# Turning the triangular inverse on VectorE and moving the sixteen spare keys of a query block, in a one-core hybrid attention and RWKV-7 block

## Chip, core and metric

One core of a Trainium2 chip runs the whole block for one batch of 512 tokens. The metric is the time of one execution on the device in microseconds (us), the median of the runs. One more execution was recorded with the hardware profiler; all rows below come from it. PE is TensorE, PEld its weight loads, DVE is VectorE, ACT is ScalarE, POOL is GpSimd, SP issues DMAs.

## What is computed

Sixteen meta tokens are put before 512 tokens of width 1024. After an RMS norm and one input projection, two branches of eight heads of 64 run beside each other and are merged by gates; a second half is a gated feed-forward net.

```python
def sb_block(q_blk, q_pos, k, v):            # stick-breaking attention
    z = einsum('bhqd,bhsd->bhqs', q_blk, k) * HEAD_DIM ** -0.5
    visible = arange(T)[None, :] < q_pos[:, None]
    nl = where(visible, softplus(z), 0.0)
    between = cumsum(nl, reverse=True) - nl
    weights = where(visible, exp(log_sigmoid(z) - between), 0.0)
    return einsum('bhqs,bhsd->bhqd', weights, v)

def step(S, inp):                            # RWKV-7, one token
    sa = einsum('bhvk,bhk->bhv', S, -kk_t)
    S = S * w_t + sa[..., None] * (kk_t * a_t)[:, :, None, :] + v_t[..., None] * k_t[:, :, None, :]
    y = einsum('bhvk,bhk->bhv', S, r_t)

merged = sigmoid(gate_sb) * (o_sb @ w_branch_sb) + sigmoid(gate_rw) * (o_rw @ w_branch_rw)
h = h + rms_norm(merged @ w_out, norm_mix_post)
f = (silu(f @ w_ffn_gate) * (f @ w_ffn_up)) @ w_ffn_down
h = h + rms_norm(f, norm_ffn_post)
```

## The kernel before

The kernel goes through four stretches. Up to about 186 us it norms, transposes and projects (26 weight units of 1024x128, each split into a high and a low part so that three fp32r products stand for one fp32 product) and prepares the operands of both branches. From 186 to 370 us lies the mix stage, which is what the change is about. Then come the late part (`LATE`: gates of the RWKV branch, group norm, remaining gate units, branch projections), the output projection and the feed-forward net.

In the mix stage four kinds of work share the engines. Their steps are written out by hand in four lists, `ORDER_PE`, `ORDER_ACT`, `ORDER_DVE` and `ORDER_POOL`; each engine runs its list in order, and steps wait for each other over the counting semaphores `mix_pe`, `mix_act`, `mix_dve`, `mix_pool`. Names are kind, number, step, as `i2.W3`.

- `i` (inv), batches 0 to 4 of two chunks of 64 tokens (the last has one): the inverse of a unit triangular 64x64 matrix for eight heads, by doubling. `A` and `L` form the matrices. At level j, `W` multiplies the matrix by the current inverse X (tile `xx`), ACT copies the product to SBUF (`w`), `Y` multiplies the transposed X by that, and DVE writes the new blocks into X under a mask (`x`, COPY_PREDICATED). The transposed X comes from `R`: PE multiplies X by an identity into PSUM, and ACT copies that to `xt` (`xt0` to `xt4`). Up to level 4, X is block diagonal in blocks of 32; at level 5 the result itself goes to `xt`, from where `SA` reads it. POOL presets X with the identity (`ident`).
- `s` (seq), nine chunks: the recurrence. `F`, `RB` form products, DVE masks them (`aak`, `ark`, `arb`), `T0` to `T2` transpose on PE, ACT copies `bh` and `kh`, DVE copies `v`, then `Z1`, `Z`, `SA`, `OUT1`, `OUT`, `S` with the copies `z`, `sa`, `out` on ACT and `decay`, `s` on DVE.
- `a` (att), four pairs of heads: scores `Q0` to `Q2`, sigmoids on ACT (`z`, `m`), masks on POOL (`b`, `c`), running products on DVE (`S`), weights on DVE (`w`, and `t` for 16 keys of each query block), transposes `X0` to `X5` with ACT copies, `X6` (four transposes of the 16 keys) with an ACT copy to `wmeta`, and `O`: two matmuls of 512 columns with the 16 keys (`vmeta`), then the 128-key tiles. A query block of 128 sees 16 + 128(i+1) keys, so 16 are left over beside whole tiles of 128; here they are the meta tokens, the last of the reversed row.
- `g` (gate), ten weight units: each is four pieces of 6 matmuls of 512 columns (`G0` to `G3`) into bank `GBANK`; ACT and DVE split the next unit (`hi`, `lo`), DVE copies the sums to `gate_raw` (`raw`), SP writes them to HBM. `u0.U` is one more gate unit of 24 matmuls.

Work of 64x64 tiles goes through `heads`, whose matmuls run on quadrants of PE: for pairs p of 2 and 3 the operand or the result lies in the other half of the partitions, which `rows` decides. That is line 1553 of the profile; 32x32 tiles (level 5) are line 1582. A logical fp32 matmul shows as two MATMUL records.

## Time and profile before

| | |
|---|---|
| median of 3 runs | 865.57 us (863.52 to 865.91) |
| the profiled execution's own time | 865.65 us |
| its span in the profile | 863.7 us |
| busy in the span: PE | 847.9 us, 98% |
| PE weight loads | 706.4 us, 82% |
| DVE | 463.9 us, 54% |
| ACT | 350.8 us, 41% |
| POOL | 104.4 us, 12% |
| PE share of the chain that ended last | 93% |
| granted TensorE clock | full speed in all 40 slices |

The page gives busy time by engine and the chain of work that ended last, followed back from the last instruction. Matmuls are pipelined, so their durations overlap; how long a row of them takes is read from start to start in the timeline. A line of the timeline is start, duration, engine, line of code, operation, tile written and tiles read, shape, count.

### The profile page before, as it was taken

To read this page: it belongs to the slowest core of one execution; us is meant where nothing else is said; L and a number is where in the kernel's file an instruction comes from. 1 tells how busy PE (TensorE), PEld (TensorE's weight loads), DVE (VectorE), ACT (ScalarE), POOL (GpSimd) and SP (SyncE) were. 2 spreads that over 40 slices of the span, in tenths; PEclk is the share of its full clock that TensorE was granted. 3 is DMA by queue.
4 is the path that set the end of the run, shared out by engine and by line. 5 is a ranking of instruction groups with operands and counts; after the bars stand their busy time and mean duration, and the time that the engine had idled before them with its cause. 6 is when DMAs were issued, how large, how long until landed. Compare 5 with 4: busy or idle time off the path is not lost.

```text
span 863.7 us, 18793 instructions
## 1 busy us (share of the span) xinstructions
PE 847.9 (98%) x8125; PEld 706.4 (82%) x8125; DVE 463.9 (54%) x593; ACT 350.8 (41%) x520; POOL 104.4 (12%) x106
## 2 busy tenths in 40 slices
...
DMA packets 109584, 82.61 MB, mean 96 GB/s; under 512 B 3471, under 2 KB 100025, under 8 KB 109258
## 3 DMA queue, kind: packets, MB, share of 16 engines
...
q14 instruction: 13, 0.11, 0.0%
...
## 4 chain that ended last, share of the span: by engine, by line
PE 93%; DVE 4%; ACT 1%; issue 1%; DMA 0%; DVEq 0%; SPq 0%; ACTq 0%
PE psum L583 48%; PE psum L1804 19%; PE psum L1553 8%; PE psum L1609 7%; PE psum L1847 2%; PE psum L1445 2%; PE psum L1727 1%; DVE w_lo L573 1%; PE psum L1744 1%; PE psum L1758 1%; DVE shift_diff L1149 1%; PE psum L1436 1%; DVE k_mod L1190 1%; DVE v_t L1154 1%; PE psum L1520 1%
## 5 line engine op out<-in xcount | busy, mean ns | idle before, releaser
L573 DVE TENSOR_TENSOR w_lo<-w_raw,w_hi 128x1024 fp32r<-128x1024 f32 x69 | 90.3, 1309 | 119.1 <-ACT w_hi L568 114.7
L583 PE MATMUL psum<-f_hi,w_hi 128*128 128x512 f32 x336 | 130.8, 389 | 0.0
L583 PE MATMUL psum<-f_lo,w_hi 128*128 128x512 f32 x336 | 130.7, 389 | 0.0
L583 PE MATMUL psum<-f_hi,w_lo 128*128 128x512 f32 x336 | 130.7, 389 | 0.0
L1391 DVE TENSOR_TENSOR w_lo<-w_raw,w_hi 128x1024 fp32r<-128x1024 f32 x44 | 53.9, 1226 | 125.5 <-ACT w_hi L1061 121.4
L1061 ACT ACTIVATE w_hi<-w_raw 128x1024 fp32r<-128x1024 f32 x44 | 46.7, 1061 | 166.6 <-PE psum L583 159.4
L568 ACT ACTIVATE w_hi<-w_raw 128x1024 fp32r<-128x1024 f32 x70 | 73.8, 1056 | 71.7 <-PE psum L1804 56.7
L583 PE MATMUL psum<-h_hi,w_hi 128*128 128x264 f32 (+2 forms) x400 | 98.2, 310 | 0.8 <-DVE w_lo L573 0.8
L583 PE MATMUL psum<-h_lo,w_hi 128*128 128x264 f32 (+2 forms) x400 | 96.5, 306 | 0.0
L583 PE MATMUL psum<-h_hi,w_lo 128*128 128x264 f32 (+2 forms) x400 | 96.4, 306 | 0.0
L583 PEld LDWEIGHTS psum<-f_hi,w_lo 128*128 128x128 f32 x336 | 63.1, 188 | 13.2
L583 PEld LDWEIGHTS psum<-f_hi,w_hi 128*128 128x128 f32 x336 | 63.1, 188 | 13.2
L583 PEld LDWEIGHTS psum<-f_lo,w_hi 128*128 128x128 f32 x336 | 63.1, 188 | 12.8
L583 PEld LDWEIGHTS psum<-h_hi,w_hi 128*128 128x128 f32 x400 | 64.7, 188 | 7.1 <-issue 1.9
L583 PEld LDWEIGHTS psum<-h_lo,w_hi 128*128 128x128 f32 x400 | 64.5, 188 | 3.8 <-issue 0.5
L583 PEld LDWEIGHTS psum<-h_hi,w_lo 128*128 128x128 f32 x400 | 64.7, 188 | 3.4
L1804 PE MATMUL psum<-w_hi,act_hi 128*128 128x512 f32 x144 | 45.7, 390 | 0.0
L1804 PE MATMUL psum<-w_hi,act_lo 128*128 128x512 f32 x144 | 45.7, 389 | 0.0
L1804 PE MATMUL psum<-w_lo,act_hi 128*128 128x512 f32 x144 | 45.6, 389 | 0.0
L1609 PE MATMUL psum<-h_hi,w_hi 128*128 128x512 f32 x80 | 35.6, 445 | 0.0
L1804 PEld LDWEIGHTS psum<-w_hi,act_hi 128*128 128x128 f32 x144 | 26.9, 188 | 5.8 <-DVE w_lo L573 0.2
L1804 PEld LDWEIGHTS psum<-w_lo,act_hi 128*128 128x128 f32 x144 | 27.0, 188 | 5.6
...
## 6 DMA issues: line engine op xcount, KB each, us to landing
...
```

The lines of the kernel that those rows point to most:

```text
L568: nc.scalar.activation(split(u)[0][:], raw[u % RAW][:], ACT.Copy).then_inc(w_hi_done, 1)
L573: nc.vector.tensor_sub(lo[:], raw[u % RAW][:], hi[:].bitcast(F32)).then_inc(w_split, 1)
L583: mm = nc.tensor.matmul(o, w[:, (w0 + i) * P:(w0 + i + 1) * P], xs[:, k, c0:c1], start=(n == 0), stop=(n == total - 1))
L1061: s_.activation(w_hi[v % SPL][:], raw[v % RAW][:], ACT.Copy).then_inc(w_hi_done, 1)
L1149: v_.tensor_sub(diff[:], st[:, 0:T], st[:, 1:T + 1]).then_inc(sh_diff, 1)
L1154: v_.scalar_tensor_tensor(dst, diff[:], vcol[:, mu:mu + 1], st[:, 1:T + 1], ALU.mult, ALU.add).then_inc(shifted, 1)
L1391: v_.tensor_sub(w_lo[v % SPL][:], raw[v % RAW][:], w_hi[v % SPL][:].bitcast(F32)).then_inc(w_split, 1)
L1445: mm = t_.matmul(o, w[:, k * P:k * P + P], xs[:, k, c0:c1], start=(k == 0 and i == 0), stop=(k == KT - 1 and i == 2))
L1553: mm = t_.matmul(psum[rows(p, hd, moved), bnk + p // 2, o0:o0 + n], w(k, p), m(k, p), start=first, stop=last, skip_group_check=True)
L1609: mm = t_.matmul(bank(GBANK), w[:, k * P:(k + 1) * P], xs[:, k, META:T], start=(k == 0 and i == 0), stop=(k == KT - 1 and i == 2))
L1804: mm = t_.matmul(bank((2 * b if at is None else at) + h), xs[:, k, P * b:P * b + P], w[:, 512 * h:512 * h + 512], start=(k == 0 and i == 0 ...
L1847: mm = t_.matmul(psum[:, s, c0:c1], w[:, k * P:k * P + P], xs[:, k, c0:c1], start=(k == 0 and i == 0), stop=(k == KT - 1 and i == 2))
```

## The change

- `R` is gone from PE, and so are the ACT copies of it. DVE turns X by one transpose instruction of its 32x32 blocks (`t0` to `t4`, from `xx` to `xt`). `heads` needs for pairs 2 and 3 the other half of the partitions, so ACT copies these, each half across, to a new tile `xt_far` (`v0` to `v4`, two copies of 64 partitions). Level 5 is written by two masked copies, into `xt` and `xt_far`. `Y` and `SA` read through `turned`.
- The 16 keys that a query block has beside its tiles of 128 are now the first of the reversed row, the block's own newest 16. The query rows that can see them are the last 16 of each block. So `X6` is two transposes instead of four, DVE spreads 16 query columns of each into `wstrip` by a mask (`x6`, in place of the ACT copy), and `O` ends with two matmuls of 64 columns where it began with two of 512. Their values (`vstrip`) are made in the preparation by four 32-column matmuls of 128 instead of two 16-column ones of 64, in each of four units, and tiles are cut 16 columns further on.
- The copies `g.raw` and `s.v` move from DVE to ACT.
- All four order lists are new. On PE, `i0.A` comes ahead of `a0.Q0`, and `u0.U` comes last, behind `s8.OUT`.

The new `ORDER_PE` stands whole; the other lists are cut to a few lines.

```diff
-ORDER_PE = order("""
-a0.Q0 i0.A i0.L g0.G0 a0.Q1 i0.W1 s0.F i0.R0 g0.G1 s0.T1 i0.Y1 a0.Q2 i0.W2 s0.T0 i0.R1 g0.G2 i0.Y2 g0.G3 i0.W3
-s0.T2 i0.R2 g1.G0 i0.Y3 g1.G1 i0.W4 i0.R3 g1.G2 i0.Y4 g1.G3 i0.W5 s0.Z i0.R4 g2.G0 i0.Y5 g2.G1 i1.A s0.SA a0.X2
...
+i0.A a0.Q0 i0.L g0.G0 i0.W1 a0.Q1 s0.F i0.Y1 g0.G1 i0.W2 a0.Q2 i0.Y2 g0.G2 i0.W3 g0.G3 i0.Y3 s0.T2 s0.T0 s0.T1
+g1.G0 i0.W4 g1.G1 i0.Y4 s0.Z g1.G2 i0.W5 g1.G3 i0.Y5 a0.X1 a0.X2 a0.X0 i1.A s0.SA i1.L a0.X4 g2.G0 a0.X3 a0.X5
+g2.G1 a0.X6 i1.W1 s0.S a1.Q0 s1.F i1.Y1 s1.RB g2.G2 i1.W2 s1.T1 s1.T2 s1.T0 a1.Q1 g2.G3 s1.Z1 i1.Y2 s1.Z g3.G0
+s1.SA i1.W3 a1.Q2 s1.OUT1 i1.Y3 g3.G1 s1.OUT i1.W4 s1.S g3.G2 s2.F i1.Y4 s2.RB a0.O i1.W5 g3.G3 i1.Y5 s2.T1
+s2.T0 s2.T2 g4.G0 s2.Z1 i2.A s2.Z i2.L s2.SA g4.G1 s2.OUT1 s2.OUT i2.W1 s2.S g4.G2 a1.X1 s3.F i2.Y1 s3.RB a1.X4
+a1.X2 a1.X0 g4.G3 a1.X6 a1.X5 s3.T0 s3.T1 s3.T2 i2.W2 a2.Q0 s3.Z1 i2.Y2 s3.Z a1.X3 g5.G0 s3.SA i2.W3 a2.Q1
+s3.OUT1 i2.Y3 s3.OUT s3.S i2.W4 a2.Q2 s4.F i2.Y4 s4.RB g5.G1 i2.W5 g5.G2 i2.Y5 s4.T0 s4.T1 s4.T2 g5.G3 s4.Z1
+i3.A s4.Z i3.L s4.SA a1.O s4.OUT1 i3.W1 s4.OUT i3.Y1 s4.S g6.G0 a2.X1 a2.X0 s5.F i3.W2 s5.RB a2.X4 g6.G1 a2.X2
+g6.G2 s5.T1 s5.T0 s5.T2 a2.X5 g6.G3 a2.X6 s5.Z1 i3.Y2 s5.Z a3.Q0 i3.W3 s5.SA a2.X3 g7.G0 s5.OUT1 i3.Y3 s5.OUT
+a3.Q1 s5.S i3.W4 g7.G1 s6.F i3.Y4 s6.RB a3.Q2 g7.G2 i3.W5 g7.G3 i3.Y5 s6.T0 s6.T1 s6.T2 a2.O s6.Z1 i4.A s6.Z
+i4.L g8.G0 s6.SA g8.G1 s6.OUT1 i4.W1 s6.OUT i4.Y1 s6.S g8.G2 s7.F i4.W2 s7.RB g8.G3 a3.X0 s7.T2 s7.T1 s7.T0
+g9.G0 s7.Z1 i4.Y2 s7.Z a3.X1 a3.X2 s7.SA i4.W3 a3.X3 s7.OUT1 i4.Y3 s7.OUT i4.W4 s7.S g9.G1 s8.F i4.Y4 s8.RB
+a3.X4 g9.G2 s8.T2 i4.W5 a3.X5 a3.X6 s8.Z1 i4.Y5 s8.Z a3.O s8.SA g9.G3 s8.OUT1 s8.OUT u0.U
...
+a0.z0 a0.m0 i0.v0 i0.w1 a0.m1 a0.z1 i0.v1 i0.w2 a0.m2 a0.z2 i0.v2 i0.w3 g0.raw s0.kh i0.v3 i0.w4 s0.bh s0.v
+g0.hi i0.v4 i0.w5 a0.x1 s0.z g1.raw a0.x0 g1.hi a0.x4 a0.x2 i1.v0 s0.sa a0.x5 i1.w1 a1.z0 a1.m0 i1.w2 i1.v1
...
+a3.x3 a3.x5 s8.z s8.sa s8.out a3.o g9.hi g9.raw
...
+i0.x0 i0.aab i0.t0 i0.x1 i0.t1 a0.S20 s0.aak a0.S21 i0.x2 a0.S10 i0.t2 a0.S11 a0.S00 a0.S01 i0.x3 a0.t2 a0.S30
+i0.t3 a0.t1 a0.t0 a0.w0 a0.S31 a0.w3 i0.x4 i0.t4 a0.w2 a0.t3 a0.w1 i0.x5 g0.lo i1.aab i1.x0 i1.t0 g1.lo s0.decay
+a0.x6 s0.s s1.arb i1.x1 s1.aak s1.ark i1.t1 i1.x2 i1.t2 s1.decay a1.S21 i1.x3 a1.S20 i1.t3 a1.w2 s1.s a1.S01
...
-        vmeta = sb("v_meta", [P, PAIRS, HD])
+        vstrip = sb("v_strips", [P, PAIRS, P])
...
+        xt_far = [sb(f"xt_far{i}", [P, 4, C]) for i in range(2)]
...
-                    s_.activation(vmeta[0:64, o, :], psum[0:64, 5, 0:HD], ACT.Copy).then_inc(v_out, 1)
+                    s_.activation(vstrip[:, o, :], bank(5, P), ACT.Copy).then_inc(v_out, 1)
...
-                        act.wait_ge(mix_pe, last_of(MIX_PE, "inv", n, (f"W{j}", f"R{j - 1}")))
+                        act.wait_ge(mix_pe, upto(MIX_PE, "inv", n, f"W{j}"))
                         s_.activation(ww[:, :, 0:m, :], sides(IB, 0, m), ACT.Copy).then_inc(mix_act, 1)
                     else:
-                        act.wait_ge(mix_pe, last_of(MIX_PE, "inv", n, (f"W{j + 1}", f"R{j}")))
-                        s_.activation(xt[n % 2][:, :, 0:m, :], sides(IB, 256, m), ACT.Copy).then_inc(mix_act, 1)
+                        act.wait_ge(mix_dve, upto(MIX_DVE, "inv", n, f"t{j}"))
+                        s_.activation(xt_far[n % 2][head(0), 0:m, :], xt[n % 2][head(1), 1, 0:m, :], ACT.Copy)
+                        s_.activation(xt_far[n % 2][head(1), 0:m, :], xt[n % 2][head(0), 1, 0:m, :], ACT.Copy).then_inc(mix_act, 1)
                 if kind == "seq":
-                    if s in ("bh", "kh"):
-                        act.wait_ge(mix_pe, last_of(MIX_PE, "seq", c, ("T0", "T1", "T2")))
-                        dst, c0 = {"bh": (bh, 0), "kh": (kh, 128)}[s]
+                    if s in ("bh", "kh", "v"):
+                        act.wait_ge(mix_pe, last_of(MIX_PE, "seq", c, ("T0", "T1", "T2") if c != LAST_C else ("T2",)))
+                        dst, c0 = {"bh": (bh, 0), "kh": (kh, 128), "v": (v_tm, 256)}[s]
                         s_.activation(by_side(dst[:]), sides(SB_, c0, 2), ACT.Copy).then_inc(mix_act, 1)
                     if s == "z":
                         act.wait_ge(mix_pe, upto(MIX_PE, "seq", c, "Z"))
@@ -924,8 +923,13 @@
                     if s == "out":
                         act.wait_ge(mix_pe, last_of(MIX_PE, "seq", c, ("OUT",) if c == LAST_C else ("OUT", "S")))
                         s_.activation(by_side(ar[:, 0, :, cols(c)]), sides(SB_, 0, 2), ACT.Copy).then_inc(mix_act, 1)
-                if kind == "gate":
+                if kind == "gate" and s == "hi":
                     hi_unit(act, U_MIX + n + 2)
+                if kind == "gate" and s == "raw":
+                    if n >= 2:
+                        act.wait_ge(gate_kept[n % 2], 16 * (n // 2))
+                    act.wait_ge(w_used, U_MIX + n + 1)
+                    s_.activation(gate_raw[n % 2][:], bank(GBANK), ACT.Copy).then_inc(mix_act, 1)
...
+                    if s[0] == "t":
+                        dve.wait_ge(mix_dve, upto(MIX_DVE, "inv", n, f"x{s[1]}"))
+                        v_.transpose(xt[n % 2][:, :, 0:m, :], xx[:, :, 0:m, :]).then_inc(mix_dve, 1)
                     if s[0] == "x":
                         j = int(s[1])
                         if j == 0:
                             dve.wait_ge(mix_pool, upto(MIX_POOL, "inv", n, "ident"))
                         else:
                             dve.wait_ge(mix_pe, upto(MIX_PE, "inv", n, f"Y{j}"))
-                        dst = xt[n % 2] if j == LEVELS - 1 else xx
                         mask = sides_of(bytes_[:, j * C:j * C + C], m)
-                        v_.copy_predicated(dst[:, :, 0:m, :], mask, sides(IB, 0 if j else 256, m)).then_inc(mix_dve, 1)
+                        new = sides(IB, 0 if j else 256, m)
+                        if j == LEVELS - 1:
+                            v_.copy_predicated(xt[n % 2][:, 0, 0:m, :], mask[:, 0], new[:, 0])
+                            v_.copy_predicated(xt_far[n % 2][:, 0:m, :], mask[:, 1], new[:, 1]).then_inc(mix_dve, 1)
+                        else:
+                            v_.copy_predicated(xx[:, :, 0:m, :], mask, new).then_inc(mix_dve, 1)
...
-                    if s == "raw":
-                        if n >= 2:
-                            dve.wait_ge(gate_kept[n % 2], 16 * (n // 2))
-                        dve.wait_ge(w_used, U_MIX + n + 1)
-                        v_.tensor_copy(gate_raw[n % 2][:], bank(GBANK)).then_inc(mix_dve, 1)
-                    else:
-                        lo_unit(dve, U_MIX + n + 2)
-                if kind == "att":
+                    lo_unit(dve, U_MIX + n + 2)
+                if kind == "att" and s == "x6":
+                    dve.wait_ge(mix_pe, upto(MIX_PE, "att", n, "X6"))
+                    if n:
+                        dve.wait_ge(mix_pe, upto(MIX_PE, "att", n - 1, "O"))
+                    last_q = bank(T_BANKS[6], 2 * P).rearrange("p (h q) -> p h q", h=2)[:, :, P - META:P]
+                    own = consts[:, K_STR:K_STR + QB].unsqueeze(1).unsqueeze(3).to_broadcast([P, 2, QB, META])
+                    v_.tensor_tensor(wstrip[:], last_q.unsqueeze(2).to_broadcast([P, 2, QB, META]), own, ALU.mult).then_inc(mix_dve, 1)
...
+                        dve.wait_ge(mix_pool, upto(MIX_POOL, "att", n, f"b{i}"))
                         if s[0] == "w":
-                            dve.wait_ge(mix_pool, upto(MIX_POOL, "att", n, f"b{i}"))
-                            w = stick[:, :, c0 + 1:c1 - META]
-                            v_.tensor_mul(w, w, rest[n % 2][:, :, c0:c1 - META - 1]).then_inc(mix_dve, 1)
+                            w = stick[:, :, c0 + META:c1]
+                            v_.tensor_mul(w, w, rest[n % 2][:, :, c0 + META - 1:c1 - 1]).then_inc(mix_dve, 1)
                         else:
                             if n:
                                 dve.wait_ge(mix_pe, upto(MIX_PE, "att", n - 1, "X6"))
-                            v_.tensor_mul(smeta[:, i, :, 0:META], stick[:, :, c1 - META:c1],
-                                          rest[n % 2][:, :, c1 - META - 1:c1 - 1]).then_inc(mix_dve, 1)
+                            v_.tensor_mul(sstrip[:, :, QB - 1 - i, 1:META], stick[:, :, c0 + 1:c0 + META],
+                                          rest[n % 2][:, :, c0:c0 + META - 1]).then_inc(mix_dve, 1)
...
-                        t_.transpose(quads(4, P)[:, b4, :], vst[o % 2][:, SEQ - P * b4 - P:SEQ - P * b4], ident)
-                    for hr in range(2):
-                        mm = t_.matmul(psum[meta_rows(hr), 5, 0:HD], vst[o % 2][:, SEQ:T], ident[:, head(hr)],
+                        t_.transpose(quads(4, P)[:, b4, :], vst[o % 2][:, T - P * b4 - P:T - P * b4], ident)
+                    for g in range(QB):
+                        mm = t_.matmul(psum[32 * g:32 * g + 32, 5, 0:P], vst[o % 2][:, P * g:P * g + 32], ident,
                                        start=True, stop=True)
...
+            def turned(b):
+                return lambda k, p, e: xt_far[b % 2][k, 2 * e + p % 2, :] if p // 2 else xt[b % 2][k, 0, 2 * e + p % 2, :]
...
-                    if s[0] in "WR":
-                        j = int(s[1]) - (s[0] == "W")
-                        pe.wait_ge(mix_dve, last_of(MIX_DVE, "inv", n, ("aab", "x0") if j == 0 else (f"x{j}",)))
+                    if s[0] == "W":
+                        j = int(s[1])
+                        pe.wait_ge(mix_dve, last_of(MIX_DVE, "inv", n, ("aab", "x0") if j == 1 else (f"x{j - 1}",)))
                         for e in steps_of(n, s):
-                            if s == f"W{LAST}":
+                            if j == LAST:
                                 mm = quarter(IB, 2 * C * e, 1, 0, 0, late_half(aab, e), early_half(xx, e))
-                            elif s[0] == "W":
+                            else:
                                 mm = heads(IB, 2 * C * e, C, 0, [(1, of_batch(aab, e), of_batch(xx, e))])
-                            else:
-                                mm = heads(IB, 256 + 2 * C * e, C, 0, [(1, of_batch(xx, e), identity)])
                     if s[0] == "Y":
                         j = int(s[1])
-                        pe.wait_ge(mix_act, last_of(MIX_ACT, "inv", n, (f"w{j}", f"xt{j - 1}")))
+                        pe.wait_ge(mix_act, last_of(MIX_ACT, "inv", n, (f"w{j}", f"v{j - 1}")))
+                        pe.wait_ge(mix_dve, upto(MIX_DVE, "inv", n, f"t{j - 1}"))
                         for e in steps_of(n, s):
                             if j == LAST:
-                                mm = quarter(IB, 2 * C * e, 0, 0, C // 2, early_half(ww, e), late_half(x_t, e))
+                                mm = quarter(IB, 2 * C * e, 0, 0, C // 2, early_half(ww, e), lambda k, p: x_t(k, p, e)[:, C // 2:C])
                             else:
-                                mm = heads(IB, 2 * C * e, C, 1, [(0, of_batch(x_t, e), of_batch(ww, e))])
+                                mm = heads(IB, 2 * C * e, C, 1, [(0, lambda k, p: x_t(k, p, e), of_batch(ww, e))])
...
-                        pe.wait_ge(mix_dve, upto(MIX_DVE, "seq", c, "v"))
+                        pe.wait_ge(mix_act, last_of(MIX_ACT, "seq", c, ("bh", "kh", "v") if c != LAST_C else ("v",)))
...
-                        mm = heads(SB_, 0, C, 1, [(0, of_batch(xt[b % 2], e), whole(z_st))])
+                        mm = heads(SB_, 0, C, 1, [(0, lambda k, p: turned(b)(k, p, e), whole(z_st))])
...
-                        for i in range(QB):
-                            mm = t_.transpose(psum[0:64, T_BANKS[k], P * i:P * i + P],
-                                              smeta[:, i].rearrange("p h k -> p (h k)"), ident)
+                        for hr in range(2):
+                            mm = t_.transpose(psum[:, T_BANKS[k], P * hr:P * hr + P],
+                                              sstrip[:, hr].rearrange("p g k -> p (g k)"), ident)
...
-                    pe.wait_ge(mix_act, last_of(MIX_ACT, "att", n, [f"x{k}" for k in range(7)]))
-                    for hr in range(2):
-                        t_.matmul(psum[head(hr), O_BANK, :], vmeta[meta_rows(hr), n, :], wmeta[meta_rows(hr), :],
-                                  start=True, stop=False)
+                    pe.wait_ge(mix_act, last_of(MIX_ACT, "att", n, [f"x{k}" for k in range(6)]))
+                    pe.wait_ge(mix_dve, upto(MIX_DVE, "att", n, "x6"))
                     for j in range(QB):
                         for hr in range(2):
                             v0 = (2 * n + hr) * HD
-                            mm = t_.matmul(psum[head(hr), O_BANK, SEQ - WIDTH[j]:SEQ], vtok[:, j, v0:v0 + HD],
-                                           rest[n % 2][:, hr, OFF[j]:OFF[j] + WIDTH[j]], start=False, stop=(j == QB - 1))
+                            t_.matmul(psum[head(hr), O_BANK, SEQ - WIDTH[j]:SEQ], vtok[:, j, v0:v0 + HD],
+                                      rest[n % 2][:, hr, OFF[j]:OFF[j] + WIDTH[j]], start=(j == 0), stop=False)
+                    for hr in range(2):
+                        last_q = psum[head(hr), O_BANK, :].rearrange("p (i q) -> p i q", q=P)[:, :, P - META:P]
+                        mm = t_.matmul(last_q, vstrip[:, n, head(hr)], wstrip[:, hr], start=False, stop=True)
...
+    f[:, K_STR:K_STR + QB] = (row // 32 == QB - 1 - np.arange(QB)[None, :]) & (row % 32 < META)
```

## Rows read from the trace of the kernel before

**Rows 1.** The page, busy time and share of the span: TensorE.

```profile
PE 847.9 (98%) x8125; PEld 706.4 (82%) x8125; DVE 463.9 (54%) x593; ACT 350.8 (41%) x520; POOL 104.4 (12%) x106
```

**Rows 2.** Busy time of each engine in five stretches, 186 to 370 us: their sum.

```profile
sum 184.00, PE 182.48 PEld 138.67 DVE 100.28 ACT 85.92 POOL 33.25; mean PE 36.50 PEld 27.73 DVE 20.06 ACT 17.18 POOL 6.65
```

**Rows 3.** Waits of TensorE, 186 to 370 us: releaser, total, times, longest.

```profile
PE psum L1727 <- ACT rest L939: 1.0, 1, 1.0
PE psum L1727 <- ACT qT L857: 0.8, 1, 0.8
```

**Rows 4.** Groups of TensorE instructions by line and form: the R steps.

```profile
L1553 PE MATMUL psum<-consts,x_inv 64*64 64x64 f32 x704 | 15.6, 219 | 0.0
```

**Rows 5.** Timeline of TensorE at 302.5 us: an R, an RB, a gate piece.

```profile
302.56 0.64 PE L1553 MATMUL psum<-consts,x_inv 64*64 64x64 f32 x32
303.02 0.41 PE L1553 MATMUL psum<-a_r,b_t 64*64 64x64 f32 x16
303.37 0.50 PE L1609 MATMUL psum<-h_hi,w_hi 128*128 128x512 f32 x1
```

**Rows 6.** Timeline of TensorE at 341.6 us: the two parts of an O.

```profile
341.59 1.07 PE L1753 MATMUL psum<-meta_weights,v_meta 16*64 16x512 f32 x4
342.60 2.37 PE L1758 MATMUL psum<-rest,v_tok 128*64 128x512 f32 x16
```

**Rows 7.** Timeline of TensorE, 353 to 359 us: transposes X2 to X5, then X6.

```profile
353.82 1.75 PE L1744 MATMUL psum<-consts,stick 128*128 128x128 f32 x14
...
358.55 0.63 PE L1747 MATMUL psum<-consts,stick_meta 128*64 128x128 f32 x4
```

**Rows 8.** Timeline of TensorE at 147.9 us: values of the 16 keys.

```profile
147.89 0.29 PE L1532 MATMUL psum<-consts,v_stage 128*16 128x64 f32 x4
148.11 0.51 PE L583 MATMUL psum<-h_hi,w_hi 128*128 128x264 f32 x2
```

**Rows 9.** Groups of VectorE, 184 to 400 us: form, count, busy, mean ns, idle before.

```profile
L1224 DVE COPY_PREDICATED x_inv<-byte_masks,psum 128x512 f32<-128x512 uint8 x20 | 14.7, 736 | 22.5 <-PE psum L1553 22.5
L1284 DVE RECIPROCAL y_rs<-y_rs 128x512 f32<-128x512 f32 x4 | 13.1, 3310 | 0.0
L1265 DVE TENSOR_TENSOR_SCAN rest<-rest 128x528 f32<-128x528 f32 x8 | 10.1, 1278 | 0.5 <-POOL rest L753 0.2 <-ACT xt L912 0.2
L1255 DVE COPY gate_raw<-psum 128x512 f32<-128x512 f32 x10 | 6.9, 688 | 11.5 <-PE psum L1609 11.5
L1238 DVE COPY v_tm<-psum 128x256 f32<-128x256 f32 x9 | 3.8, 420 | 10.0 <-ACT bh L917 5.9 <-ACT kh L917 2.6 <-PE psum L1553 1.1
```

**Rows 10.** Groups of ScalarE, 184 to 400 us, same columns as rows 9.

```profile
L912 ACT ACTIVATE xt<-psum 128x512 f32<-128x512 f32 x20 | 11.9, 597 | 13.3 <-PE psum L1553 13.0
L917 ACT ACTIVATE kh<-psum 128x256 f32<-128x256 f32 x8 | 3.1, 390 | 3.9 <-PE psum L1553 3.7
L948 ACT ACTIVATE meta_weights<-psum 64x512 f32<-64x512 f32 x4 | 2.4, 589 | 1.7 <-PE psum L1747 1.7
L965 ACT ACTIVATE y_sq<-a_r 128x512 f32<-128x512 f32 x4 | 2.3, 621 | 0.0
```

**Rows 11.** The chain that ended last, 362 to 384 us: start, length, work.

```profile
361.98 2.78 PE psum L583 x12
...
368.45 0.40 PE psum L1553 x8
...
368.90 0.94 PE psum L1553 x38
...
369.86 0.39 ACT a_r L926
...
370.30 3.70 PE psum L1775 x8
```

**Rows 12.** Timeline, 403 to 410 us: the low part of the RWKV result, its first reader.

```profile
403.80 3.39 POOL L769 TENSOR_TENSOR orw_lo<-y_o,orw_hi 128x512 fp32r<-128x512 f32 x2 [3.10 <-ACT orw_hi L974]
...
408.06 0.39 PE L583 MATMUL psum<-orw_lo,w_hi 128*128 128x512 f32 x1
```

More of the change, by code:

```diff
@@ L637, in _ @@
                 if 0 <= i < EARLY:
-                    sp.wait_ge(mix_dve, upto(MIX_DVE, "gate", i, "raw"))
+                    sp.wait_ge(mix_act, upto(MIX_ACT, "gate", i, "raw"))
                     sp.dma_start(kept[i], gate_raw[i % 2][:]).then_inc(gate_kept[i % 2], 16)
@@ L1615, in steps_of @@
             def steps_of(b, step):
-                level = int(step[1]) + (step[0] == "R")
-                return [e for e, c in enumerate(BATCHES[b]) if c or level <= FIRST_LEVELS]
+                return [e for e, c in enumerate(BATCHES[b]) if c or int(step[1]) <= FIRST_LEVELS]
             for kind, n, s in ORDER_PE:
```

95 lines of the change are left out of this document (36 added, 59 removed).

## The prediction

> **What bounds the kernel now.** I read the page first: TensorE is busy 98% of the span [rows 1], and the chain of work that ended last lies on it for 93%. Then the stretches. From 186 to 370 us, where the change acts, PE is busy 182.48 of 184.00 us, DVE 100.28, ACT 85.92 [rows 2]. Ends of matmuls are modelled, so busy time can hide waits; two views tell. The waits of PE name two, 1.0 and 0.8 us, both in the first 5 us of the stretch [rows 3]. And the timeline, read from start to start, puts one PE step behind the other: an R over two chunks, 32 records, takes 303.02 - 302.56 = 0.46 us, 14.4 ns a record, the same as its neighbours [rows 5]. So in this stretch PE sets the time, and what PE is spared counts, unless it turns into waiting. DVE and ACT wait mostly for PE [rows 9, 10].
>
> **R leaves PE.** The 704 records [rows 4] are 19 steps of 32 and 6 of 16: 19 x 0.46 + 6 x 0.23 = 10.1 us [rows 5]. Gain 10.1.
>
> By the Trainium skill (TensorE: Matmul & The Clock Gate, Part 1, "Wait - 56ns, not 53.3ns?") starts of matmuls never follow each other in less than about 25 ns. By that rule R would cost 704 x 25 = 17.6 us, and the estimate would be 7.5 us lower. The trace does not agree: 14.4 ns on quadrants, so the sum stays with the row.
>
> **O ends with strips.** The two 512-column products with 16 keys take 342.60 - 341.59 = 1.01 us [rows 6], four times: 4.0. The new ones have 64 columns, an eighth: 0.13 us if they go side by side as the old ones, 0.26 if not. They come last and not first, which moves nothing else. Gain 4 x (1.01 - 0.13) = 3.5 us, at least 3.0.
>
> **X6 is two transposes.** 14 transposes take 1.75 us; X6 takes 0.63 us for four, so ten more cost 1.12, 0.11 each [rows 7]. Two less, four times: gain 0.9 us (0.8 to 0.9).
>
> **Preparation of the 16 keys' values.** Before: four records of 64 columns, 148.11 - 147.89 = 0.22 us [rows 8]. After: eight of 128 columns, in four column groups. A 512-column fp32 record alone takes 3.70 / 8 = 0.46 us [rows 11], 0.9 ns a column. Serial that is 8 x 128 x 0.9 = 0.92 us, four side by side 0.23. The old pair of 512 columns ran two side by side (1.01 us for four records, where 1.85 is serial) [rows 6]. Loss per unit 0.0 to 0.7; two side by side gives 0.24 more, but the new ones are half as wide, so I take 0.15. Four units: loss 0.6 us (0 to 2.9).
>
> **The order on PE.** Between a 64-wide step and a wide one PE loses some 0.11 us: RB's 16 records take 0.35 to the next gate piece, not 0.23 [rows 5]. Counted through the two lists, 121 such neighbours become 113: gain 0.9 us (0 to 1.5). At the start, `i0.A` (0.5 us) now runs while PE waits 0.8 us for the copy of `qT` [rows 3]: gain 0.5. The wait of `a0.Q1` for the two sigmoids stays. At the end, PE waits from about 369.8 to 370.30 for the ACT copy of the last `OUT` [rows 11]; `u0.U`, 24 matmuls, now lies there. The eight records of OUT1 take 0.45 us, where eight at 14.4 ns are 0.12, and with `a3.O` and a gate piece on both sides of SA that wait should go too [rows 11]. Gain 0.5 + 0.3 = 0.8 (0.4 to 0.8).
>
> **What moves to DVE and ACT.** No row shows a DVE transpose. Its lower bound is 0.42 us, the COPY of half the elements; its upper bound the scan of 528, 1.28 us; far out stands the reciprocal of 512 with 3.31 us [rows 9]. It reads and writes 512 elements once, like the COPY of 512 at 0.69 us, and I take that, 0.42 for 256. The skill says of it (Vector Engine (DVE) Microarchitecture Reference, 3.8) that it sustains one element per cycle and lane; that would be about the COPY's time, and no row here shows it. DVE gets 20 x 0.69 + 5 x 0.42 = 15.9 us of transposes, 0.8 for level 5 written in two parts, 1.1 for `x6`, and loses 6.9 (`raw`) and 3.8 (`v`) [rows 9]: +7.1. ACT loses 11.9 + 5 x 0.39 for `xt` and 2.4 for `wmeta`; it gets 20 x 2 x 0.41 + 5 x 2 x 0.30 = 19.4 for `v0` to `v4` (0.39 for 256 elements from PSUM, and SBUF as source costs 0.02 more: 0.62 against 0.60), 10 x 0.60 for `raw`, 9 x 0.39 for `v`: +12.7 [rows 10]. In a stretch of about 169 us that is 107 us for DVE (64%) and 99 for ACT (58%), both under PE.
>
> What decides is the path of a level: from the end of Y to the next Y. Before: x 0.74, W and R 0.92, the copies w and xt 1.2, so 2.9 us and crossings. After: x 0.74, t 0.69, v 0.82, with W and w beside them: 2.3 and crossings. That is shorter at 0.69 a transpose, and longer from 1.3. The new waits have work queued behind them: on ACT `v_j` waits for DVE with `w`, `kh` and the gate's `hi` behind it; `raw` waits for the end of the unit and for the store of two units ago; on DVE `x6` waits for PE with `s0.s` or a `lo` behind it, and O and the next Q0 now wait for it. `t` of the attention waits for POOL's `b` as well, but X waits for all of them anyway. SP's store of a gate waits for ACT now, and the next loads stand behind it; `raw` and `hi` stand side by side in the list, so this moves loads by about 1 us, with two units of cover.
>
> The new list has less filler on PE, and both other engines are fuller, so I add waits of 2.2 us (0 to 9; the upper end is what the second rival costs).
>
> **Behind the stretch.** Unit 1 needs the split of `g9`, which ACT and DVE do beside `u0.U` (24 x 2.78 / 12 = 5.6 us [rows 11]). The low part of the RWKV result is ready at 403.80 + 3.39 = 407.19 and first read at 408.06 [rows 12]: 0.9 us to spare. ACT will start on the late part about 3 us earlier against PE, since `u0.U` comes behind the recurrence, so this does not get worse. I cost it at nothing; without that cover it is under 1 us. Output projection and feed-forward are untouched.
>
> **Sum.** -10.1 - 3.5 - 0.9 + 0.6 - 0.9 - 0.5 - 0.8 + 2.2 = -13.9 us. The profiled execution has a span of 863.7 us and took 865.65 us, so 1.95 lies around the span; its time stands 0.1 us above the median of 865.57. 863.7 - 13.9 = 849.8, plus 1.95: 851.7 us, 1.6% less than now.
>
> **Rivals.**
> First: the level's path gets too long. A transpose at the scan's 1.28 us puts 0.6 us into each level. In the new list 11 of 25 levels have no gate piece between W and Y (for example `i1.W1 s0.S a1.Q0 s1.F i1.Y1`); there it shows, 6.6 us in place of the 2.2 that I added, and DVE's queue slips with 12 us more: 856 to 859. For it: no row has the price, and DVE's queue also holds eight scans a head pair. Against it: gate pieces of 6 x 0.23 us and more stand in the other levels.
>
> Second: the R steps were filler. PE waits at the same places for ACT and DVE, and the 10.1 us come back as waits: 851.7 + 10.1 = 861.8. For it: in a tight chain a removed step only shows a wait. Against it: the waits of PE in the middle of the stretch are near nothing, and the paths get shorter.
>
> Third, on the other side: DVE becomes the bound of the stretch. Without transposes DVE has 91.5 us there. At the reciprocal's 3.31 us they add 20 x 3.31 + 5 x 1.7 = 75, and 166 us at the most that an engine in such a weave reaches, some 85%, make 196 in place of 184: 877 us. It decides from where (91.5 + 22.5 t) / 0.85 = 184, t = 2.9 us a transpose. The skill's sentence above speaks against it, and so does that the reciprocal alone is that slow in rows 9.
>
> **How the numbers follow.** Forecast 0.70, its own range 847 to 855.5. First rival 0.17, second 0.07, third 0.06. The range of 8 in 10 takes in the first rival and leaves out the other two, with a little above and below: 847 to 859. A measurement of this kernel tells 0.3%, 2.6 us, from no change. Faster: forecast, first rival and most of the second, 0.92. Same 0.03, slower 0.05.
>
> **What would show it.** PE records fall by 704 for R, 8 for X6, and rise by 16 in the preparation. The stretch from Q0 to the first gate matmul of the late part shrinks from 184.1 to about 169. `t` shows as a DVE transpose of about 0.69 us over 512 elements, the two `xt_far` copies at 0.41. The strips of O take 0.13 to 0.26. PE's waits list stays short; a list with ACT `xt_far` or DVE `xt` at over 5 us means the first rival, one with the recurrence's copies the second. If a transpose takes over 1.3 us, or the preparation shows more than 1 us, my sum is wrong there.

## The result, and the profile after

| | before | after |
|---|---|---|
| median of the runs | 865.5 us (863.52 to 865.91, 4 runs) | 850.76 us (850.64 to 852.15, 4 runs) |
| profiled execution, its span | 865.65 us, 863.7 us | 852.15 us, 850.1 us |

The ratio is 0.9838, with a 95% interval of 0.982 to 0.9856: 1.6% faster. The forecast was 851.7 us, range 847 to 859. What follows shows that the sum was 1.0 us too good, and that a difference in the kernel's first 20 us, outside the change, hid it.

The page's busy line, the busy time of the changed kernel's mix stage, 184.78 to 356.80 us, and of 186 to 370 us (length; busy time and count of PE, its weight loads, DVE, ACT, POOL; granted clock; DMA share and GB/s), and the waits of PE from 184 to 352 us:

```profile
PE 834.1 (98%) x7429; PEld 695.5 (82%) x7429; DVE 470.0 (55%) x608; ACT 365.9 (43%) x560; POOL 102.4 (12%) x106
```

```profile
184.78:356.80 172.02, 169.31 (x3938) 128.39 (x3937) 107.22 (x185) 104.22 (x204) 33.55 (x53) 1.00 0.16 49
186.00:370.00 184.00, 181.35 (x3948) 135.88 (x3949) 117.16 (x189) 112.23 (x214) 38.61 (x55) 1.00 0.18 55
```

```profile
PE psum L1733 <- ACT rest L943: 0.7, 1, 0.7
PE psum L1557 <- POOL k_t L745: 0.7, 1, 0.7
PE psum L1557 <- DVE arb L1241: 0.2, 1, 0.2
PE psum L1557 <- ACT w_inv L907: 0.2, 1, 0.2
```

PE is as full as before, with 696 records fewer [rows 1, 2], which is 704 and 8 less and 16 more, as predicted. In the mix stage DVE is busy for 107 us, as the sum had it, and ACT for 104, where it had 99; 3.0 us of that are two steps of the late part (`osb_hi`, `y_sq`), which now run beside `u0.U`. The second row, up to 370 us, takes in 13.2 us of the late part, so it can't be set against rows 2. The list of waits names 1.8 us [rows 3].

Groups of DVE and ACT, columns as in rows 9:

```profile
L1219 DVE STREAM_TRANSPOSE xt<-x_inv 128x512 f32<-128x512 f32 x20 | 14.1, 703 | 0.4
L1219 DVE STREAM_TRANSPOSE xt<-x_inv 128x256 f32<-128x256 f32 x5 | 2.2, 434 | 0.0
L1261 DVE TENSOR_TENSOR strip_weights<-psum,consts 128x128 f32<-128x128 f32 x4 | 1.2, 289 | 3.9 <-PE psum L1753 3.9
...
L911 ACT ACTIVATE xt_far<-xt 64x256 f32<-64x256 f32 x20 | 8.3, 416 | 0.2
L910 ACT ACTIVATE xt_far<-xt 64x256 f32<-64x256 f32 x20 | 8.3, 416 | 10.4 <-DVE xt L1219 10.1
```

The transpose takes 703 and 434 ns (0.69 and 0.42 had been taken), each copy across 416 (0.41). That is 1.05 ns an element and lane, (703 - 434) / 256, above a fixed 0.17 us; the plain copies of 512 and 256 elements, 688 and 420 ns, give 1.05 ns as well [rows 9]. The Trainium skill (Vector Engine (DVE) Microarchitecture Reference, 3.8) has the transpose sustain one element per cycle and lane; that its slope is the plain copy's agrees with it.

**Where the time went.** I measure one stretch in every kernel: from the start of the last projection record on PE (184.78 below) to the start of the first gate record of the late part (line 1782). The time of a step is the distance from its first record to the next step's.

```profile
184.78 0.39 PE L585 MATMUL psum<-h_hi,w_lo 128*128 128x512 f32 x1
185.10 0.69 PE L1557 MATMUL psum<-a_r,b_t 64*64 64x64 f32 x32
185.86 1.13 PE L1733 MATMUL psum<-kT,qT 64*128 64x512 f32 x4
...
189.28 0.69 PE L1557 MATMUL psum<-x_inv,aab 64*64 64x64 f32 x32
190.64 0.61 PE L1733 MATMUL psum<-kT,qT 64*128 64x400 f32 x2 [0.67 <-ACT rest L943]
...
356.80 3.60 PE L1782 MATMUL psum<-sig_xg,gate_up_w 128*128 128x512 f32 x8
```

The stretch is 356.80 - 184.78 = 172.0 us; before it was 370.30 - 185.01 = 185.3. So 13.3 us less. Summed by kind of step over both traces:

| steps | before | after | difference |
|---|---|---|---|
| R, 25 | 12.92 | 0 | -12.92 |
| A, L, W, Y | 29.17 | 32.75 | +3.58 |
| recurrence (F, RB, T, Z1, Z, SA, OUT1, OUT, S) | 34.62 | 37.41 | +2.79 |
| gate pieces, 40 | 64.06 | 63.30 | -0.76 |
| O, 4 | 13.23 | 9.67 | -3.56 |
| X6, 4 | 1.76 | 1.15 | -0.61 |
| other X, and Q | 22.15 | 21.75 | -0.40 |
| before the first step, u0.U, wait behind OUT | 7.38 | 5.99 | -1.39 |
| sum | 185.29 | 172.02 | -13.27 |

Outside it, the preparation takes 0.5 us more (163.5 to 164.0 us from the 61st record to the last projection record), and what lies behind the stretch 0.15 us less. Together 12.9 us less, where the forecast had 13.9.

**Why the medians differ by 14.7 us all the same.** The first matmuls do not run at the same pace in each execution. Busy time from 15.4 to 20.6 us (the same columns) of before, of after and of e7 below:

```profile
15.40:20.60 5.20, 4.92 (x25) 4.96 (x26) 4.87 (x7) 2.34 (x5) 2.43 (x9) 1.00 1.13 296
```

```profile
15.40:20.60 5.20, 5.07 (x31) 5.10 (x32) 4.89 (x7) 2.90 (x6) 1.72 (x9) 1.00 1.05 308
```

```profile
15.40:20.60 5.20, 5.04 (x43) 5.08 (x44) 4.90 (x8) 3.44 (x8) 1.64 (x9) 1.00 1.11 322
```

The same engine, busy throughout, starts 25, 31 and 43 records there. Two like records of before show both paces:

```profile
18.68 0.42 PE L1445 MATMUL psum<-h_lo,w_hi 128*128 128x264 f32 x1
...
20.59 0.28 PE L1445 MATMUL psum<-h_lo,w_hi 128*128 128x264 f32 x1
```

The cause is the granted clock, although its column says 1.00 in all three. The column counts what the trace's entries of the clock take away, and these entries begin only at 20.08 us in before, at 18.65 in after and at 14.30 in e7; ahead of the first one it prints 1.00 for want of an entry. The pace changes right there: in before the 128-column records follow each other every 0.21 us up to 19.96 and every 0.11 from 20.13, half the time, which is the step between the two levels of 1.2 and 2.4 GHz. All 14 traces agree. Where the entries begin by 14.3 us, the 61st record starts at 19.4 to 19.5; where they begin at 18.65 to 20.14, PE has been at work since 15.5 us at the lower level, and the 61st record starts at 20.8 to 21.6. In before that is 4.5 us at half pace, so 2.3 us late by this estimate, and 2.15 measured; in after it is 3.1 us, so 1.6, and 1.4 measured. In every trace PE is at work up to 14.1 to 14.5 us and then waits 1.2 to 1.5 us; the level rose ahead of that pause in five traces (13.65 to 14.30 us) and behind it in nine. What decides between the two stays open.

Whatever comes later shifts by that. With the quickest start, before would take 865.65 - 2.15 = 863.5 us, its fastest run, and after 852.15 - 1.4 = 850.75, its median: 12.8 us apart, which is the 12.9 of the trace. This is an estimate, since only the profiled executions show their start. A median of four runs of this kernel can be off by some 1.5 us for this alone, so below the stretch is what I compare. It comes from one profiled execution of each kernel. Where two traces run the same work it repeats well: from the 61st to the last projection record ten of the eleven kernels with the new preparation take 163.96 to 164.02 us, the eleventh (e10) 164.33. But the start is not all that varies: e5's ten runs spread over 4.0 us, and e2's fastest is 1.0 us below its profiled one, which had the quick start already.

### The profile page after: what moved, and what is told of

It reads as the page before. It is cut to its first block, busy times and chain, and to the rows that moved or that the text cites. A ratio compares the mean times of both kernels' runs of the same rounds, so it can differ in the third digit from the quotient of the medians.

```text
span 850.1 us, 17495 instructions
## 1 busy us (share of the span) xinstructions
PE 834.1 (98%) x7429; PEld 695.5 (82%) x7429; DVE 470.0 (55%) x608; ACT 365.9 (43%) x560; POOL 102.4 (12%) x106
## 4 chain that ended last, share of the span: by engine, by line
PE 88%; DVE 5%; ACT 3%; issue 2%; POOL 1%; DMA 0%; DVEq 0%; SPq 0%; POOLq 0%; ACTq 0%
PE psum L585 48%; PE psum L1811 19%; PE psum L1557 6%; PE psum L1616 5%; PE psum L1854 2%; PE psum L1449 2%; DVE w_lo L575 1%; PE psum L1750 1%; PE psum L1733 1%; PE psum L1762 1%; DVE shift_diff L1150 1%; PE psum L1440 1%; DVE k_mod L1191 1%; DVE v_t L1155 1%; ACT rest L943 1%
## 5 line engine op out<-in xcount | busy, mean ns | idle before, releaser
L585 PEld LDWEIGHTS psum<-f_hi,w_lo 128*128 128x128 f32 x336 | 63.1, 188 | 13.2
L1811 PEld LDWEIGHTS psum<-w_hi,act_lo 128*128 128x128 f32 x144 | 27.0, 188 | 5.6
```

The costliest lines, as they stand in the source:

```text
L585: mm = nc.tensor.matmul(o, w[:, (w0 + i) * P:(w0 + i + 1) * P], xs[:, k, c0:c1], start=(n == 0), stop=(n == total - 1))
L1811: mm = t_.matmul(bank((2 * b if at is None else at) + h), xs[:, k, P * b:P * b + P], w[:, 512 * h:512 * h + 512], start=(k == 0 and i == 0 ...
```

## The experiments

Each set of four (e1 to e4, e5 to e8, e9 to e12) ran beside the kernel before, whose median was 864.1, 864.6 and 865.5 us; a ratio below is to that one. Stretches and starts are of one profiled execution each.

| kernel | median us | 61st record at | stretch |
|---|---|---|---|
| before | 864.1, 864.6, 865.5 beside the three sets | 21.6 | 185.3 |
| after | 850.8 | 20.8 | 172.0 |
| e1_inverse_only | 858.3 | 19.4 | 179.8 |
| e2_strips_only | 863.0 | 19.4 | 184.1 |
| e3_copies_only | 864.0 | 20.9 | 185.1 |
| e4_old_order | 857.8 | 21.1 | 177.3 |
| e5_r_unread | 862.9 | 21.0 | 181.3 |
| e6_t_twice | 856.5 | 21.1 | 176.3 |
| e7_ends_back | 855.2 | 19.4 | 174.3, and 1.8 behind it |
| e8_table_early | 850.6 | 20.9 | 170.9 |
| e9_ends_back_raw_first | 853.6 | 19.5 | 173.3, and 0.8 behind it |
| e10_copies_back | 853.6 | 19.4 | 173.9 |
| e11_strips_x6_early | 862.2 | 21.6 | 181.9 |
| e12_best | 851.3 | 21.4 | 171.5 |

**e1: the inverse alone, old order.**

```diff
-a0.Q0 i0.A i0.L g0.G0 a0.Q1 i0.W1 s0.F i0.R0 g0.G1 s0.T1 i0.Y1 a0.Q2
+a0.Q0 i0.A i0.L g0.G0 a0.Q1 i0.W1 s0.F g0.G1 s0.T1 i0.Y1 a0.Q2
```

> The kernel before with the new inverse alone (R out of PE, the turn on DVE, two copies on ACT), in the old order. Theory, PE sets the time of this stretch and what it is spared counts: 704 records less, 10.1 us, less a little for the path of a level, so -8 to -10 us, 856 to 857.5 us. Rival, the R steps only filled gaps: no gain, 864 to 866 us, with the 10 us to be seen as waits of PE. Rival, the transposes lie open: gain under 5 us, with waits of PE for DVE.

Measured: ratio 0.9936 (0.9919 to 0.9954), stretch -5.5 us. The R steps had taken 12.9 us, of which 10.1 are their records and 2.8 the changes from a 64-wide to a wide step behind them. Those changes stay, since another 64-wide step now stands there (`s0.F` to the next step 0.23 us before, 0.34 now). So by the sum's own price 10.1 were to be had, and 4.6 came back as waits:

```profile
PE psum L1736 <- ACT rest L940: 1.0, 1, 1.0
PE psum L1736 <- ACT qT L857: 0.8, 1, 0.8
PE psum L1620 <- DVE gate_raw L1263: 0.7, 2, 0.5
PE psum L1561 <- ACT w_inv L909: 0.5, 2, 0.3
PE psum L1561 <- DVE x_inv L1232: 0.5, 1, 0.5
PE psum L1784 <- ACT a_r L927: 0.5, 1, 0.5
PE psum L1561 <- DVE s_st L1257: 0.5, 2, 0.3
PE psum L1561 <- DVE v_tm L1246: 0.3, 1, 0.3
PE psum L1561 <- DVE aab L1216: 0.2, 1, 0.2
```

Against rows 3 this list has 2.7 us of new waits (all but `rest`, `qT` and `a_r`), spread over six releasers, none above 0.5 us at once. The other 1.9 us are below what the list names. My expectation (-8 to -10) was wrong: in the old order nearly half of the R records had stood in front of something that was only just ready.

**e2, e11: the strips alone, old order.** In e2 DVE's list had `i2.x2 g4.lo i2.x3 a1.x6 s3.decay`; in e11:

```diff
-i2.x2 g4.lo i2.x3 a1.x6 s3.decay
+i2.x2 a1.x6 g4.lo i2.x3 s3.decay
```

> The kernel before with the strips for the 16 keys alone (O, X6 and the preparation of the key values), in the old order. Theory: -3.5 for O, -0.9 for X6, +0.6 for the preparation, so -3.8 us, 861.7 us. If x6 on DVE holds up O or the next Q0, the gain is smaller: 862.5 to 865 us and a wait of PE for DVE of 0.5 us or more at each of four units.

> The kernel before with the strips alone, and a1.x6 ahead of g4.lo and i2.x3 in DVE's list, not behind them. Theory: the 1.1 us that PE waited at a2.Q0 for strip_weights go, 1.1 us less in the stretch from the last projection record to the late gates (184.1 to 183.0 us). The three gaps of 0.45 to 0.5 us inside steps of 64-column records, that no semaphore explains, are what else that run lost; if they are tied to the place in the program, they stay.

Measured: e2 0.9988 (0.9978 to 0.9997), stretch -1.15; e11 0.9959 (0.9944 to 0.9974), stretch -3.35. In both O gave 3.56 and X6 0.79, as in the sum. e2's 863.0 us lies in the range that was given for a held-up `x6` (862.5 to 865), but with one wait and not four. What e2 lost is in its waits and its timeline:

```profile
PE psum L1731 <- DVE strip_weights L1260: 1.1, 1, 1.1
```

```profile
283.15 0.30 PE L1556 MATMUL psum<-a_r,b_t 64*64 64x64 f32 x8
283.73 0.35 PE L1556 MATMUL psum<-a_r,b_t 64*64 64x64 f32 x8 [0.28 <-issue]
```

The next unit's Q0 waited 1.1 us for `a1.x6`, a DVE instruction of 0.29 us whose input had been there for almost 7 us (X6 at 267.3, `a1.x6` at 274.5): it stood in line behind `i2.x3`, which waits for PE. Two places up in the list, that wait is gone. The rest are three stops of 0.45 to 0.5 us in the middle of a step, between records that wait for nothing (one is shown), and one of 0.3 us in `i3.R4` at 326.4. In e11 two of the three are gone, which is why its stretch fell by 2.2 us and not by the 1.1 expected; the one at 283.5 stays (0.53), and that in `i3.R4` is 0.59 there. The changed kernel has none of this size. What makes them stays open. They need not belong to the edit: e9 below has one of 0.50 us at 248.2 in a step that e7 runs without, and the two differ only in the last six entries of ACT's list, which run 100 us later. No kernel's stretch was seen twice, so how much of e2's loss is the kernel's and how much that execution's isn't shown.

**e3, e10: the copies alone.** e3 moves `g.raw` and `s.v` to ACT in the old order; e10 moves them back to DVE in the new one.

```diff
-                    s_.activation(gate_raw[n % 2][:], bank(GBANK), ACT.Copy).then_inc(mix_act, 1)
+                        v_.tensor_copy(gate_raw[n % 2][:], bank(GBANK)).then_inc(mix_dve, 1)
```

> The kernel before with only the gate's and the value's copies moved from DVE to ACT. Theory: neither engine is the bound, so nothing changes, within 1 us of the kernel before (864.5 to 866.5 us). Rival: ACT's queue gets in PE's way, 867 us or more; or DVE was a bound in places, 863 us or less.

> The changed kernel with the copies of the gate and of the value back on DVE, at the places in its list that their times on ACT give; everything else new. Theory by the sum of the prediction: DVE goes from 64 to some 70% of the stretch, ACT down; nothing is a bound, 0 to +1 us. Rival: in the new order the transposes make DVE's queue the tight one, the copies behind it are late, +2 to +4 us, with waits of PE for DVE.

Measured: e3 0.9998 (0.9988 to 1.0008), stretch -0.2, as expected. e10 is 1.8 us worse in the stretch than after, 853.6 against 850.8 in the medians, and 2.2 us in the span against the other runs of after, whose start by their time was as quick (850.9 to 848.7). PE waits for DVE where it did not, or did for 0.2 us:

```profile
PE psum L1562 <- DVE arb L1235: 0.8, 1, 0.8
PE psum L1738 <- ACT rest L937: 0.7, 1, 0.7
PE psum L1562 <- POOL k_t L744: 0.7, 1, 0.7
PE psum L1621 <- DVE gate_raw L1257: 0.6, 1, 0.6
```

Of the 2.2 us, 0.4 lie ahead of the stretch, where the two kernels run the same work. So the same move is worth nothing without the transposes and about 2 us with them, though DVE with the copies is busy for only 117 of the 174 us of its stretch (67%). The expectation by busy share (0 to +1) was wrong; the rival's (2 to 4) is at its lower edge. One reservation: the new places of the copies in DVE's list were set by their times on ACT, and another list might do better.

**e4: everything but the order.** The four lists of before, with the steps that went and came.

> Everything the change does to the work (inverse, strips, copies), but in the order of the kernel before. Theory: the sum without the terms of the order (-0.9 for neighbours, -0.5 start, -0.8 end), so about -11.5 to -12 us, 853.5 to 854 us, and 2.5 to 3.5 us above the changed kernel. If the parts lean on the new order (DVE's and ACT's queues), it is more: 857 us or above, with waits of PE for DVE or ACT. If the new order is worth nothing, 851 us.

Measured: 0.9928 (0.991 to 0.9946), stretch -8.0 us, 5.2 us above the changed kernel's. The second case held: the parts lean on the order. Three of its waits:

```profile
PE psum L1732 <- DVE strip_weights L1260: 1.9, 1, 1.9
...
PE psum L1556 <- DVE s_st L1251: 0.8, 3, 0.3
...
PE psum L1556 <- DVE x_inv L1231: 0.5, 1, 0.5
```

1.9 of the 5.2 us are the placement of `a1.x6` again, which is mine and not the old order's. In e11 it cost nothing once moved; that was not tried here, so that the new order proper is worth 3 to 4 us is an estimate. The sum had 2.2 for it (0.9, 0.5 and 0.8).

**e5: R back on PE, unread, new order.**

```diff
+                    if s[0] == "W":
+                        for e in steps_of(n, s):
+                            mm = heads(IB, 256 + 2 * C * e, C, 0, [(1, of_batch(xx, e), identity)])
```

> The changed kernel with the 704 R records put back on TensorE, behind each W; nothing reads their result, and w waits for them as before. The inverse goes on with the DVE transpose. Theory: in the new order PE sets the time too, so the 10.1 us come back, 859.5 to 861.5 us if the changed kernel is at 850.5. The old order gave back 5.5 of them only; if the new order has idle time in which R fits, as that one had, the loss is 5 to 7 us (856 to 858 us). Rival, R was filler: under 2 us more.

Measured: 862.87 us (860.7 to 864.7), stretch +9.3 us. The median lies above the range expected (859.5 to 861.5), the profiled execution, 861.54 us, at its end; the ten runs spread over 4.0 us, more than the start explains, and what else varies isn't shown. For the second rival the answer is the same by either number: in the new order nearly all of the 10.1 us are on the path. The stretch also prices the record: 9.3 / 704 = 13 ns. By the Trainium skill (TensorE: Matmul & The Clock Gate, Part 1, "Wait - 56ns, not 53.3ns?") 704 starts could not come in under 17.6 us, an estimate from its figure of about 25 ns; the measurement disagrees, for 64x64 records that spread over quadrants.

**e6: each DVE transpose issued twice.**

```diff
+                        if turns:
+                            dve.wait_ge(again, turns)
+                        v_.transpose(turned_again[:, :, 0:m, :], xx[:, :, 0:m, :]).then_inc(again, 1)
+                        turns += 1
```

> The changed kernel with each of the 25 DVE transposes issued twice, the first into a tile that nobody reads, ahead of the real one: 0.70 us more into each level and 16 us more on DVE. Theory: in the new order most levels have other work between Y and Y; PE waits 1 to 4 us more, 852 to 855 us. First rival (the level's path is as good as open): 6 us or more, 857 us and above. If the cover is full: within 1 us.

Measured: 856.54 us (856.0 to 856.8), stretch +4.2 us: above the 852 to 855 expected and just below the first rival's 857. The two instructions overlap, so from the start of the first to the end of the second a turn takes 1.30 us, 0.60 more than one alone. That is the first rival made real, since it had assumed 1.28 and said 856 to 859. At 0.70 us it does not apply. Of the 4.2 us, 0.6 are a stop as in e2, at 251.3; of 13.5 us more in the 25 turns some seven tenths are hidden. The longest waits:

```profile
PE psum L1564 <- DVE s_st L1259: 1.3, 3, 0.6
PE psum L1564 <- ACT w_inv L909: 1.3, 4, 0.4
```

The waits are for the recurrence's state and for `w_inv`, not for the transposes themselves: the level's delay is passed on.

**e7, e9: the two ends put back.** `i0.A` behind `a0.Q0`, `u0.U` ahead of `s8.SA`; e9 also lets ACT copy the last gate sooner.

```diff
-i0.A a0.Q0 i0.L
+a0.Q0 i0.A i0.L
...
-s8.Z a3.O s8.SA g9.G3 s8.OUT1 s8.OUT u0.U
+s8.Z a3.O u0.U s8.SA g9.G3 s8.OUT1 s8.OUT
```

and on ACT in e9:

```diff
-s8.z s8.sa s8.out a3.o g9.hi g9.raw
+s8.z a3.o s8.sa s8.out g9.raw g9.hi
```

> The changed kernel with i0.A behind a0.Q0 again and u0.U ahead of s8.SA again, the rest of the new order as it is. Theory: 0.5 us at the start and 0.5 at the end come back, +1.0 us (0.8 to 1.3). Rival: i0.A and u0.U cover nothing else late, no difference.

> The run with i0.A and u0.U at their old places, where PE waited 2.4 us for the copy gate_raw, with one more edit: ACT's list ends a3.o s8.sa s8.out g9.raw g9.hi in place of s8.sa s8.out a3.o g9.hi g9.raw. Theory, the late copies of ACT are what u0.U covers: the wait falls to 0.9 to 1.1 us (two short copies after OUT), 1.4 us gained, and if the low clock behind the wait came from its length, the 1.8 us of it go too: 1.4 or 3.2 us less than that run from the last projection record to the end. Rival: no change, and something else holds the late part.

Measured: e7 855.19 us, stretch +2.2 and 1.8 behind it, 4.1 in all where +1.0 was expected; e9 853.61 us. The start of it gives nothing: Q1 begins 5.9 us after the last projection record with `i0.A` ahead (190.64 - 184.78) or behind, since it waits for the sigmoids. All of it is the end. The wait of PE, then three windows (the same columns), of e7:

```profile
PE psum L1781 <- ACT gate_raw L931: 2.4, 1, 2.4
```

```profile
357.00:359.00 2.00, 1.35 (x3) 0.68 (x4) 1.23 (x1) 1.97 (x3) 0.00 (x0) 1.00 0.27 100
359.00:361.00 2.00, 2.00 (x4) 0.92 (x3) 0.00 (x0) 2.00 (x5) 1.38 (x1) 0.51 0.34 96
361.00:363.00 2.00, 2.00 (x4) 0.73 (x4) 0.96 (x1) 1.98 (x3) 2.00 (x1) 0.64 0.26 73
```

and the same of e9:

```profile
PE psum L1780 <- ACT gate_raw L930: 1.0, 1, 1.0
```

```profile
359.00:361.00 2.00, 2.00 (x6) 0.95 (x5) 0.00 (x0) 2.00 (x5) 1.40 (x1) 1.00 0.10 30
361.00:363.00 2.00, 2.00 (x7) 1.13 (x6) 0.98 (x1) 1.98 (x3) 2.00 (x1) 1.00 0.23 65
```

The change put `g9.raw` last in ACT's list, behind a 1.06 us split. PE waits for all of that before the late part, 2.4 us, and behind that wait the granted clock is at its lower level, 1.2 GHz, from 359.05 to 362.46 us (0.51 and 0.64 in the two windows): 1.8 us more. With `u0.U` last, its 5.7 us of matmuls cover these copies. In e9 the wait is 1.0 us and the clock stays at 1.00, as expected. Still only 1.9 of the 4.1 us come back: 0.9 in the stretch, where 1.4 at the end meet the stop of 0.5 at 248.2, and 1.0 behind it, where PE now waits at 392.2 for a weight's low part from DVE, which costs 0.7. So that the late copies are what `u0.U` covers is shown. Its move gains 0.5 us against the kernel before and saves 4 us that the new order would have lost without it.

**e8, e12: a version that beats both?** e8 loads the sigmoid's table in an idle stretch of ACT. e12 adds three swaps of neighbours.

```diff
+                if u == N_IN - 2:
+                    act.wait_ge(n_dve, 1)
+                    s_.activation(small[:, 30:31], small[:, 5:6], ACT.Sigmoid).then_inc(n_rs, 1)
```

```diff
-s2.OUT1 s2.OUT i2.W1
+s2.OUT1 i2.W1 s2.OUT
...
-s8.SA g9.G3 s8.OUT1 s8.OUT u0.U
+s8.SA s8.OUT1 g9.G3 s8.OUT u0.U
...
-s0.bh a0.c0 a0.b0 a0.c3 s0.kh
+s0.bh s0.kh a0.c0 a0.b0 a0.c3
```

> The changed kernel with one added sigmoid of one element on ACT in an idle stretch before the recurrence, so that the table of the sigmoid is loaded there and not at 187.4 us, where PE waits 0.7 us for the two sigmoids. Theory: -0.7 us (-0.5 to -0.9), with the first Q1 no longer late. Rival: something else is late at the same place, or the table is changed back before: no difference.

> The changed kernel with the early table load, i2.W1 between s2.OUT1 and s2.OUT, g9.G3 between s8.OUT1 and s8.OUT (so that OUT doesn't wait for the end of OUT1), and on POOL s0.kh right behind s0.bh. Theory: -1.1 us as the early table showed in the stretch, -0.3 for each OUT1, -0.5 for the wait at s0.T1: the stretch from 172.2 to some 170 us, the time 848.5 us (848 to 850). Rival: freed work meets the next wait, and only the 1.1 us stay.

Measured: e8 850.64 us (850.0 to 851.6), stretch -1.1; e12 851.25 us (850.1 to 852.3), stretch -0.5. The table load moved and Q1 starts 0.7 us sooner. In e12 two of the three swaps did at their place what they should (`s2.OUT1` 0.52 to 0.18 us, `i0.Y3` to the next step 1.35 to 0.51). At the third, `s8.OUT1` takes 0.38 in place of 0.52, but `s8.SA` 0.97 in place of 0.39, as OUT1 now waits for SA's copy (`sa_st` below). The rest was lost at the next steps:

```profile
PE psum L1559 <- ACT w_inv L909: 1.0, 2, 0.9
PE psum L1559 <- ACT sa_st L924: 0.5, 1, 0.5
PE psum L1559 <- POOL k_t L744: 0.4, 1, 0.4
```

e8's stretch gained 1.1 us where 0.7 was expected for it; e12's 170 us and 848.5 us were missed, and not even the 1.1 us of its rival stayed. Neither kernel is told from the changed one by its time.

## Why the prediction was right, and where it was not

- What bounds the kernel, and rival 2: right in the new order (e5, +9.3 of 10.1), half right in the old one (e1, 5.5). Start-to-start times show what a step takes, not that its removal is free of waits; that needed the new order.
- R, order and waits were -10.1 - 0.9 + 2.2 = -8.8 in the sum. The steps concerned (R, A to Y, recurrence, gates, other X and Q) changed by -7.7. Here the sum was off by 1.1 us.
- Part of it is a step that failed: "that wait should go too" of OUT1. The eight records still take 0.53 us when OUT follows directly:

```profile
349.77 0.79 PE L1557 MATMUL psum<-a_r,s_st 64*64 64x64 f32 x10
350.30 0.27 PE L1557 MATMUL psum<-ark,v_tm 64*64 64x64 f32 x2
```

  It is no wait for SA's copy, as I had it. OUT waits for the completion of OUT1 on PE itself (line 1713 of the changed kernel). Work beside SA doesn't help, work between OUT1 and OUT does (0.18 us in e12). Over the kernel OUT1 rose from 1.96 to 2.74 us: the new order puts the two side by side twice and not once (0.34 more), and at `s3` and `s5`, where `i2.Y3` and `i3.Y3` follow, OUT1 takes 0.36 and 0.60 us to the next step.
- O -3.56 for -3.5, the four strip records of the last O taking 0.22 us to the next step (347.56 to 347.78 in the timeline). X6 -0.61 for -0.9. Preparation +0.5 for +0.6, `v_stage` eight records in 147.48 - 147.12 = 0.36 us against 0.22 [rows 8].
- Start: `i0.A` under the wait for `qT` gained nothing for Q1, since the table load of 1.28 us stood behind it (e7, e8). The sum's 0.5 came from elsewhere: `i0.W1` now runs in the wait for the sigmoids.
- End: the ACT wait of 0.5 us went, as said. That the move of `u0.U` had only this effect was luck: what lies behind was costed at nothing, "without that cover it is under 1 us". The cover was worth 4 us (e7).
- Rival 1: its price was right at 1.30 us a turn (e6), its condition not met; from where between 0.70 and 1.30 it starts was not tried. Rival 3, a transpose of 2.9 us or more, is out at 0.70; that an engine reaches 85% at the most was an assumption of it that no run tested.
- The copies had no term of their own: with DVE and ACT "both under PE" they were to gain nothing. That holds in the old order (e3), and misses some 2 us in the new one (e10).
- The predicted time came within 0.9 us of the median because two errors offset, which is luck: 1.0 us too much gain in the sum, and a start 2.15 us slower than the quickest in the profiled execution that the sum was made against. R, O and the strips are right in kind and nearly in size, so luck is in the last 1 us only.
